# Order of pieces, gate drain and side work in a three-layer fp32 block: one planner, four edits

## The chip, the cores and the metric

One core of a Trainium2 chip. The time is that of one execution on the device, in microseconds (us); the kernel before and the kernel after are compared by the median of their runs.

## The reference

512 tokens of width 1024 pass a layer of dilated attention, a layer of differential attention, and a hybrid block (feed-forward, a mix of sparse attention, state space and memory attention, feed-forward). All is float32. What the change touches:

```python
# first layer: three groups of 16 heads, merged by their log-denominators
alpha = jax.nn.softmax(jnp.stack(lses, axis=0), axis=0)
o = jnp.sum(alpha[..., None] * jnp.stack(outs, axis=0), axis=0)
y = o.reshape(B, S, DIL_WIDTH) * jax.nn.silu(gate)
return y @ w_out                                # 1024 x 1024
# second layer: eight heads of width 128
o = rmsnorm(o, subln) * (1.0 - lambda_init)
y = o.reshape(B, S, DIFF_WIDTH) * jax.nn.silu(gate)
return y @ w_out                                # 1024 x 1024
# hybrid block, of the memory tokens alone
mem_kv = rms_norm(mem, mem_norm[l]) @ w_mem_kv[l]
```

Each layer ends with `h = h + rmsnorm(y, norm_post)`, and the next one normalises `h` again.

## The kernel before, in words

A planner (`make_plan`, with `Plan` from line 100 on) writes one list of jobs. Each engine walks the same list in order and does its own part of each job, so the order of the list is the order of the work on every queue; semaphores tie the engines together.

**Panels, steps, pieces.** A dense product is a *panel* of 512 output columns in four PSUM banks (`panel`, L135). Its weights come in *pieces* of two 128-row chunks (`piece`, L121), 0.5 MB each. A *step* takes two pieces, and has one `mac` job for each of the four banks (token blocks or feature blocks); every yield of the generator is one `mac`. The layers' inputs and these weights are split into a high and a low fp32r part, and a product is three matmuls: high by high, high by low, low by high. So one `mac` of a step of two pieces is 12 matmuls.

**The way of a piece.** SyncE loads it into one of four slots of `raw_ring` (`sync_program`, L1053), once the piece four before has been lowered, or, if that one is not split, once its step has ended. ScalarE rounds it into `hi_ring` (L2173) when the step that used that place of the ring has ended; GpSimd lowers it, that is, subtracts and writes `lo_ring` (L2530). Both do this at fixed places of the job list: the `mac` with the bank `look_at` of each step, up to piece number `ahead` (the pieces planned so far plus `look`).

**End of the first layer** (`dilated_layer`, L365). Under the gate's two panels runs a side stream of attention, loads and the first tile's weights; it is advanced 2.5 places a `mac` (`interleave`, L174). `first_heads` (L443) ends with the jobs `mix_ratio`, `mix_weight` and `mix_scale` of token tile 0. A gate bank is drained by ScalarE's tanh (L2180) and VectorE (L1530). Then for each token tile: VectorE computes the groups' weights (L1658 to L1671), scales two of three groups (L1678; for tile 0 all three) while ScalarE scales the third in 20 operations (L2398), sums the groups (L1688, L1690) and multiplies with the gate (L1695); TensorE transposes the tile (L1130, 8 matmuls); ScalarE rounds it (L2256) and VectorE lowers it (L1601). The projection's first panel takes one token block per tile. Between them TensorE does the memory's product with `w_mem_kv` (`memory_products`, L482; plain fp32, L1222), in four steps of one unsplit piece, and `warm` jobs: matmuls of constants whose result nobody reads (L1424). Each plain fp32 matmul shows as two records.

**End of the second layer** (`differential_layer`, L504). Attention heads are weighed by VectorE (L1749), transposed on TensorE (`turn_head`, L1433), rounded by ScalarE (L2428) and lowered by VectorE (L1755). Heads 0 to 3 come ahead of the projection's first step (K chunks 0 to 3), heads 4 to 7 between its four `mac` jobs; the second step waits for all of them.

**Side work of the first feed-forward** (`before_hybrid`, L611): 62 places that are advanced one a `mac` in ten hidden panels (80 `mac` jobs): memory's keys (L1232), the bias table (L1238), its DMA to and from memory (L2622, L2650) and eight bias heads (L1272), coefficient and table parts on VectorE, state-space tables (L1252, L1260), eight placement DMAs (L2630).

Of the kernel before, what the change touches and what calls it, by code (L numbers as in the profile page):

```python
# [12 lines left out]
NT = S // P  # L13
KC = D // P
KP = 2
# [69 lines left out]
MEM_LOOK = 2  # L85
VALUE_LEAD, HEAD_RATIO = 3, 2.0

Job = namedtuple("Job", "kind at n use")
# [5 lines left out]
class Plan:  # L94
# [23 lines left out]
        self.jobs.append(Job(kind, at, n, use))  # L118
        return use

    def piece(self, w, k0, kq, c0, n, parted, halves, wide):  # L121
        slot = len(self.pieces) % RAW
        self.slot_landed[slot] += 16 * halves
        home, prior = None, None
        if parted and wide is None:
            home = self.n_ring % SPLIT
            prior, self.last_of[home] = self.last_of[home], len(self.steps)
            self.n_ring += 1
        elif parted:
            home = SPLIT + wide  # L130
        self.pieces.append(Piece(w, k0, kq, c0, n, parted, self.n_split, len(self.steps), halves, self.slot_landed[slot], home, prior))
        self.n_split += 1 if parted else 0
        return len(self.pieces) - 1

    def panel(self, kind, w, c0, cols, form, at=(), K=KC, src="x", k_first=0, halves=1, after=(), base=0, late=((),) * 4,  # L135
              wide=(), look=(2, 2, 2), look_at=(0, 0, 0), order=None, needs=None):
        parted = src in ("x", "hidden")
        pi, n = len(self.panels), self.count["panel", kind]
        self.count["panel", kind] += 1
        use = tuple(self.fill(base + b) for b in range(4))  # L140
        if needs is not None:
            pass
        elif src != "x":
            needs = (after,) * 4
        elif form == "feature":
            needs = (tuple(v for part in self.parts for v in part),) * 4
        else:
            needs = self.parts
        self.panels.append(Panel(kind, at, n, w, cols, K, form, src, use, needs, base, late))
        for first in range(0, K, 2 * KP):  # L150
            s, last = len(self.steps), first + 2 * KP >= K
            pieces = [self.piece(w, k_first + k, min(KP, K - k), c0, cols, parted, halves, wide[k // KP] if wide else None)
                      for k in (first, first + KP) if k < K]
            if last:
                end = (f"filled{base + 3}", use[3])
            else:
                self.n_step += 1
                end = ("stepped", self.n_step)
            m = first // (2 * KP)
            self.steps.append(Step(pi, pieces, first, last, end, len(self.pieces) + look[m], look_at[m]))  # L160
            for b in range(4 if order is None else 0):
                self.job("mac", s, b)
                yield MAC_TIME if parted else RAW_TIME
# [201 lines left out]
def dilated_layer(plan, begun):  # L365
# [77 lines left out]
    def first_heads():  # L443
        plan.job("mix_load")
        for m in range(FIRST_HEADS):
            if m % 2 == 0 and m < 8:
                plan.job("mem_weigh", m // 2)
            yield
        plan.job("mix_ratio", 0)
        plan.job("mix_weight", 0)  # L450
        plan.job("mix_scale", 0)

    interleave(gate_panels(plan, w, 9 * D, 0), chain(side, first_heads()), GATE_RATIO)
    plan.job("row", "post0")
    plan.job("gain", "pre1")
    needs = [(), (), (), ()]
    main = plan.panel("y", "dil_w_out", 0, 512, "tile", at=(0,), look=(2, 6), look_at=(2, 0), needs=needs)
    memory = memory_products(plan)
    for n in range(NT):
        if n + 1 < NT:  # L460
            plan.job("mix_ratio", n + 1)
        plan.job("mix_sum", n)
        if n + 1 < NT:
            plan.job("mix_weight", n + 1)
        if n < 2:
            next(memory)
# [15 lines left out]
def memory_products(plan):  # L482

    for first in range(0, KC, KP):
        p = plan.piece("w_mem_kv", first, KP, 0, 512, False, 1, None)
        s, last = len(plan.steps), first + KP >= KC
        use = tuple(plan.fill(b) for b in (2, 3)) if first == 0 else use
        if last:
            end = ("filled3", use[1])
        else:  # L490
            plan.n_step += 1
            end = ("stepped", plan.n_step)
        plan.steps.append(Step(None, [p], first, last, end, len(plan.pieces) + MEM_LOOK, 0))
        plan.job("mem_kv", s, use)
        if last:
            plan.job("mem_out", use)
        yield
# [6 lines left out]
def differential_layer(plan):  # L504
# [52 lines left out]
    def turn_head(h):  # L557
        return ((f"drained{4 + h % 4}", plan.job("o_turn", h, banks=(4 + h % 4,))[0]),)
# [51 lines left out]

def before_hybrid(plan):  # L611
    plan.job("mem_fetch")
    for _ in range(3):
        yield
    for n in range(2):
        plan.job("mem_keep", n)
        yield
        yield
        plan.job("mem_keys", n, banks=(6,))
        yield  # L620
    plan.job("bias_table", banks=(4, 5))
    yield
    plan.job("coefficients")
    for i in range(COEF_PARTS):
        plan.job("coef_part")
# [6 lines left out]
    for _ in range(TABLE_PARTS):  # L632
        plan.job("table_part")
        yield
    for _ in range(4):
        yield
    for f in range(2):
        plan.job("k_make", f, banks=(4, 5))
# [183 lines left out]
def program(nc, I, out):  # L822
    ctx = ExitStack()
    with ctx:  # L824
# [250 lines left out]
        def tensor_program(T):  # L1075
# [4 lines left out]
            def mac(s, b, half=None):  # L1080
# [1701 lines left out]
```

## Time and profile before

| | |
|---|---|
| median of 3 runs | 2210.07 us (2203.17 to 2214.13) |
| the profiled execution | 2206.05 us |
| its span, first to last instruction | 2204.2 us |
| mean granted TensorE clock | 0.989 |
| TensorE busy | 2117.1 us |
| VectorE, ScalarE, GpSimd busy | 967.0, 866.5, 840.0 us |

PE is TensorE's matmul, DVE VectorE, ACT ScalarE, POOL GpSimd, SP SyncE. Times in timelines are us from the span's start. In a timeline a row is one instruction or a run of like ones: start, duration from the first start to the last end, engine, line, operation, output and input names, shapes and number; in brackets the idle time of the engine just before it and what ended that. The ends of matmuls are modelled. A granted clock of 1.00 is 2.4 GHz, 0.50 is 1.2 GHz.

### The profile page before, as it was taken

How to read it: one execution, taken by the hardware profiler on the slowest of the kernel's cores; microseconds unless marked ns; L12 is line 12 of the kernel's file. 1: busy time of each engine (PE TensorE's matmuls, PEld its weight loads, DVE VectorE, ACT ScalarE, POOL GpSimd, SP SyncE). 2: the span in 40 equal slices, each digit the busy share in tenths (PEclk: the TensorE clock that was granted, in tenths of full speed). 3: DMA queues.
4: the chain of work that ended last, by engine and by line, in shares of the span. 5: the costliest groups of instructions: out<-in, count | busy, mean ns of one | idle time of the engine just before them, and what ended most of it. 6: DMA issues, size and time to landing. Idle time of an engine off the chain costs nothing. (4 is left out here: it accounts for less than half of the span.)

```text
span 2204.2 us, 26734 instructions
## 1 busy us (share of the span) xinstructions
PE 2117.1 (96%) x10366; PEld 1684.7 (76%) x10366; DVE 967.0 (44%) x1642; ACT 866.5 (39%) x1769; POOL 840.0 (38%) x447
## 2 busy tenths in 40 slices
PE   8999999999899999989999999999999899999998
PEld 6788888887658767678778888787774478888886
DVE  2444645444444575654571311258666532111211
ACT  4554556564344565543331232333322232221221
POOL 4433233332333323353444445344333152444442
PEclk9999999999999999999999999999999999999999
DMA  6313233232622212132433333233344242323321
GB/s 220 96 58 96 58 96 97 77 97 78 222 92 73 88 58 77 51 122 77 134 96 107 90 101 105 83 93 99 104 149 130 85 153 67 96 96 96 96 96 58
DMA packets 130204, 218.67 MB, mean 99 GB/s; under 512 B 8712, under 2 KB 58552, under 8 KB 129872
## 3 DMA queue, kind: packets, MB, share of 16 engines
q1 hardware_dynamic: 111152, 169.68, 25.3%
q0 software_dynamic: 8096, 28.93, 4.1%
q10 hardware_dynamic: 10832, 18.35, 2.4%
q8 instruction: 84, 1.38, 0.3%
q14 instruction: 40, 0.33, 0.0%
HBM read 198.29 MB, written 18.04 MB: 98 GB/s over the span
## 5 line engine op out<-in xcount | busy, mean ns | idle before, releaser
L2530 POOL TENSOR_TENSOR lo_ring<-raw_ring,hi_ring 128x1024 fp32r<-128x1024 f32 (+1 forms) x288 | 694.5, 2434 | 1009.2 <-ACT hi_ring L2173 1009.1
L1117 PE MATMUL bank<-xh,hi_ring 128*128 128x512 f32 (+1 forms) x1568 | 610.7, 389 | 3.6 <-DVE xl L1601 2.9
L1117 PE MATMUL bank<-xh,lo_ring 128*128 128x512 f32 (+1 forms) x1568 | 593.9, 379 | 0.0
L1117 PE MATMUL bank<-xl,hi_ring 128*128 128x512 f32 (+1 forms) x1568 | 592.6, 378 | 0.0
L2173 ACT CAST hi_ring<-raw_ring 128x1024 fp32r<-128x1024 f32 (+1 forms) x288 | 288.1, 1045 | 406.5 <-PE bank L1117 385.3
L1117 PEld LDWEIGHTS bank<-xh,hi_ring 128*128 128x128 f32 x1568 | 297.1, 189 | 66.2 <-issue 13.8
L1117 PEld LDWEIGHTS bank<-xh,lo_ring 128*128 128x128 f32 x1568 | 296.5, 189 | 56.4
L1117 PEld LDWEIGHTS bank<-xl,hi_ring 128*128 128x128 f32 x1568 | 297.2, 190 | 52.7 <-issue 2.2
L1117 PE MATMUL bank<-hi_ring,xh 128*128 128x512 f32 (+1 forms) x512 | 209.4, 409 | 9.7 <-DVE xl L1755 4.9
L1117 PE MATMUL bank<-hi_ring,xl 128*128 128x512 f32 (+1 forms) x512 | 201.5, 394 | 0.0
L1117 PE MATMUL bank<-lo_ring,xh 128*128 128x512 f32 (+1 forms) x512 | 201.2, 393 | 0.0
L2187 ACT COPY arena<-bank 32x512 f32<-32x512 f32 x256 | 148.1, 579 | 63.1 <-DVE arena L1539 60.4
L1545 DVE SCALAR_TENSOR_TENSOR arena<-arena,bank 128x512 f32<-128x512 f32 x44 | 30.1, 686 | 256.4 <-ACT arena L2204 256.4
L1117 PEld LDWEIGHTS bank<-hi_ring,xh 128*128 128x128 f32 x512 | 105.1, 205 | 34.7 <-issue 14.1
L1564 DVE SCALAR_TENSOR_TENSOR x<-bank,x 128x512 f32<-128x512 f32 x40 | 27.7, 691 | 232.1 <-PE bank L1117 232.1
L1117 PE MATMUL bank<-hi_ring,hidden_hi 128*128 128x512 f32 x320 | 127.0, 397 | 0.0
L1117 PE MATMUL bank<-lo_ring,hidden_hi 128*128 128x512 f32 x320 | 126.8, 396 | 0.0
L1117 PE MATMUL bank<-hi_ring,hidden_lo 128*128 128x512 f32 x320 | 126.8, 396 | 0.0
L1117 PEld LDWEIGHTS bank<-hi_ring,xl 128*128 128x128 f32 x512 | 105.2, 205 | 18.0
L1117 PEld LDWEIGHTS bank<-lo_ring,xh 128*128 128x128 f32 x512 | 105.6, 206 | 15.7 <-issue 0.2
L2538 POOL TENSOR_TENSOR small<-small,minus_half 128x1 f32<-128x1 f32 (+2 forms) x48 | 40.2, 838 | 162.2 <-DVE small L1606 122.1
L2287 ACT COPY arena<-bank 128x512 f32<-128x512 f32 (+6 forms) x97 | 49.3, 508 | 86.6 <-PE bank L1272 21.2
(289 smaller groups left out, 2675.2 us busy)
## 6 DMA issues: line engine op xcount, KB each, us to landing
raw_ring<-in_ffn_w_in SPq DMA_DIRECT2D x176, 256.0 KB, 3.1
raw_ring<-in_dil_w_in SPq DMA_DIRECT2D x80, 512.0 KB, 3.6
raw_ring<-in_ffn_w_out SPq DMA_DIRECT2D x44, 512.0 KB, 3.7
raw_ring<-in_diff_w_in SPq DMA_DIRECT2D x32, 512.0 KB, 3.7
raw_ring<-in_w_in SPq DMA_DIRECT2D x32, 512.0 KB, 3.6
arena<-scratch_heads POOLq DMA_DIRECT2D x4, 1584.0 KB, 12.0
scratch_gates<-arena ACTq DMA_DIRECT2D x24, 256.0 KB, 2.0
arena<-scratch_gates POOLq DMA_DIRECT2D x24, 256.0 KB, 5.0
```

What stands on the lines that cost most here:

```text
L1117: ins = T.matmul(bank[pb][:, cols if p.form == "feature" else slice(0, p.cols)], lhsT, rhs, start=(k == 0 and m == 0 and half != 1), stop= ...
L1545: V.scalar_tensor_tensor(ff_e[:, o, :], ff_e[:, o, :], 1.0, psum, ALU.add, ALU.mult).then_inc(drained[o], 1)
L1564: V.scalar_tensor_tensor(dst, psum, 0.25 if p.kind == "down" else 0.5, dst, ALU.mult, ALU.add).then_inc(drained[o], 1)
L2173: A.copy(split_home(q)[0][:, 0:q.kq * q.n], raw_ring[:, p % RAW, 0:q.kq * q.n]).then_inc(rounded, 1)
L2187: ins = A.copy(rope_b[32 * quad:32 * quad + 32, o % 2, :], psum[32 * (quad ^ 1):32 * (quad ^ 1) + 32, :])
L2287: A.copy(dst, src).then_inc(drained[b], 1)
L2530: G.tensor_tensor(lo, raw_ring[:, p % RAW, 0:q.kq * q.n], hi.bitcast(F32), ALU.subtract).then_inc(lowered, 1)
L2538: G.tensor_tensor(dst, dst, minus_half[:, 0:dst.shape[-1]], ALU.pow).then_inc(made_, 1)
```

## The change

Four edits of the job list. (1) The projection's first two pieces of the first layer are planned ahead of memory's four (`ready`, with their step number given), memory's steps no longer look two pieces ahead, and the `warm` jobs shrink from 5, 9 and 9 matmuls (tiles 0, 2, 3) to 4 and 4 (tiles 2, 3). (2) `mix_scale` of tile 0 comes after the gate's last drain. (3) The side work of the feed-forward gets more empty places. (4) In the second layer heads 2 and 3 are weighed at steps 20 and 21 (were 21 and 23), the projection's first panel has four steps of one piece (two heads) with waits by step, and two `mac` jobs of the first two heads go between the later transposes.

```diff
@@ piece, panel
-    def piece(self, w, k0, kq, c0, n, parted, halves, wide):
+    def piece(self, w, k0, kq, c0, n, parted, halves, wide, step=None):
+        step = len(self.steps) if step is None else step
@@
-              wide=(), look=(2, 2, 2), look_at=(0, 0, 0), order=None, needs=None):
+              wide=(), look=(2, 2, 2), look_at=(0, 0, 0), order=None, needs=None, ready=None, per=2):
@@
-        for first in range(0, K, 2 * KP):
-            s, last = len(self.steps), first + 2 * KP >= K
+        for first in range(0, K, per * KP):
+            s, last = len(self.steps), first + per * KP >= K
             pieces = [self.piece(w, k_first + k, min(KP, K - k), c0, cols, parted, halves, wide[k // KP] if wide else None)
-                      for k in (first, first + KP) if k < K]
+                      for k in range(first, min(K, first + per * KP), KP)] if ready is None or first else ready
@@ dilated_layer
-        plan.job("mix_scale", 0)
 
     interleave(gate_panels(plan, w, 9 * D, 0), chain(side, first_heads()), GATE_RATIO)
+    plan.job("mix_scale", 0)
     plan.job("row", "post0")
     plan.job("gain", "pre1")
     needs = [(), (), (), ()]
-    main = plan.panel("y", "dil_w_out", 0, 512, "tile", at=(0,), look=(2, 6), look_at=(2, 0), needs=needs)
+    ready = [plan.piece("dil_w_out", k, KP, 0, 512, True, 1, None, len(plan.steps) + KC // KP) for k in (0, KP)]
+    main = plan.panel("y", "dil_w_out", 0, 512, "tile", at=(0,), look=(2, 6), look_at=(2, 0), needs=needs, ready=ready)
@@
-        if n != 1:
-            plan.job("warm", n, 4 + 2 * (n % 2), 5 if n == 0 else 9)
+        else:
+            plan.job("warm", n, 4 + 2 * (n % 2), 4)
@@ memory_products
-        plan.steps.append(Step(None, [p], first, last, end, len(plan.pieces) + MEM_LOOK, 0))
+        plan.steps.append(Step(None, [p], first, last, end, len(plan.pieces), 0))
@@ differential_layer
-        if step >= 17 and step % 2:
-            plan.job("o_weigh", (step - 17) // 2)
+        if step in (17, 19, 20, 21):
+            plan.job("o_weigh", (17, 19, 20, 21).index(step))
+    ready = [turn_head(h) for h in range(3)]
+    plan.job("o_lower", 0)
     run_all(side)
+    ready.append(turn_head(3))
+    for h in range(1, 4):
+        plan.job("o_lower", h)
@@
-    ready = [turn_head(h) for h in range(4)]
-    for h in range(4):
-        plan.job("o_lower", h)
     for h in range(4, 8):
         plan.job("o_weigh", h)
-    plan.parts = (sum(ready, ()),) * NT
-    late = [(), (), (), ()]
-    main = plan.panel("y", "diff_w_out", 0, 512, "tile", at=(0,), late=late, look=(2, 6))
+    plan.parts = (ready[0] + ready[1],) * NT
+    late = {2: ready[2] + ready[3]}
+    main = plan.panel("y", "diff_w_out", 0, 512, "tile", at=(0,), late=late, look=(2, 2, 4, 6), look_at=(0, 0, 0, 0), per=1)
     ready = []
     for h in range(4, 8):
-        next(main)
+        for _ in range(2 if h < 6 else 1):
+            next(main)
         ready.append(turn_head(h))
         plan.job("o_lower", h)
-    late[:] = [sum(ready, ())] * NT
+    late[4], late[6] = ready[0] + ready[1], ready[2] + ready[3]
@@ before_hybrid: yields
 mem_fetch, then          3 -> 8
 mem_keep, then           2 -> 3   (for each of two)
 bias_table, then         1 -> 3
 last table part, then    4 -> 8
@@ mac
-                    for name_value in p.late[b]:
+                    for name_value in (p.late.get(st.k0, ()) if isinstance(p.late, dict) else p.late[b]):
```

## Rows read from the trace of the kernel before

**Rows 1.** The page, part 1: busy us, share of the span, instructions.
```profile
PE 2117.1 (96%) x10366; PEld 1684.7 (76%) x10366; DVE 967.0 (44%) x1642; ACT 866.5 (39%) x1769; POOL 840.0 (38%) x447
```
**Rows 2.** TensorE's waits, whole span: us in total, times, longest.
```profile
PE bank L1272 <- DMA arena<-scratch_bias: 3.0, 2, 2.3
...
PE bank L1232 <- DVE arena L1767: 1.0, 1, 1.0
```
**Rows 3.** Timeline of TensorE, end of the first layer.
```profile
597.22 9.56 PE L1222 MATMUL bank<-raw_ring,arena 128*128 128x512 f32 x16 [4.67 <-DVE arena L1530]
606.62 4.46 PE L1424 MATMUL bank<-consts 128*128 128x512 f32 x10
...
611.78 7.03 PE L1222 MATMUL bank<-raw_ring,arena 128*128 128x512 f32 x16
...
622.83 0.77 PE L1117 MATMUL bank<-hi_ring,xh 128*128 128x512 f32 x1 [3.14 <-POOL lo_ring L2530]
...
638.88 7.88 PE L1424 MATMUL bank<-consts 128*128 128x512 f32 x18
646.60 1.04 PE L1130 MATMUL bank<-consts,arena 128*128 128x128 f32 x8
```
**Rows 4.** Windows: stretch, length, busy us (records) by engine, granted clock, DMA, GB/s.
```profile
597.20:606.60 9.40, 9.38 (x16) 4.07 (x17) 7.33 (x14) 5.12 (x21) 0.00 (x0) 0.74 0.80 302
622.80:627.50 4.70, 4.36 (x12) 3.06 (x13) 4.60 (x6) 1.20 (x5) 3.19 (x1) 0.65 0.60 176
...
940.00:963.30 23.30, 17.05 (x83) 13.45 (x82) 16.58 (x31) 9.26 (x21) 6.99 (x6) 0.93 0.28 91
963.30:974.30 11.00, 10.97 (x48) 9.12 (x49) 0.81 (x2) 6.18 (x10) 11.00 (x5) 1.00 0.51 150
```
**Rows 5.** Timeline of VectorE, end of the first layer.
```profile
592.98 3.50 DVE L1678 TENSOR_TENSOR arena<-arena,small 128x1024 f32<-128x1024 f32 x3
596.39 0.68 DVE L1530 SCALAR_TENSOR_TENSOR arena<-arena,bank 128x512 f32<-128x512 f32 x1
...
600.74 1.22 DVE L1695 SCALAR_TENSOR_TENSOR arena<-arena 128x1024 f32<-128x1024 f32 x1
...
605.83 0.24 DVE L1658 TENSOR_REDUCE small<-arena 128x16 f32<-128x48 f32 x1 [1.87 <-issue]
...
613.73 1.22 DVE L1695 SCALAR_TENSOR_TENSOR arena<-arena 128x1024 f32<-128x1024 f32 x1
...
620.52 3.25 DVE L1690 TENSOR_TENSOR arena<-arena 128x1024 f32<-128x1024 f32 x1
```
**Rows 6.** Timeline of ScalarE, end of the first layer.
```profile
600.86 4.88 ACT L2398 ACTIVATE arena<-arena,small 128x64 f32<-128x64 f32 x20 [3.08 <-DVE small L1671]
611.55 1.07 ACT L2256 CAST xh<-bank 128x512 fp32r<-128x512 f32 x2 [5.81 <-PE bank L1130]
```
**Rows 7.** GpSimd's timeline there, and one DMA row (KB, us to landing).
```profile
582.42 3.12 POOL L2590 DMA_DIRECT2D arena<-scratch_heads  x4 [6.09 <-DMA scratch_heads<-arena]
...
619.76 6.23 POOL L2530 TENSOR_TENSOR lo_ring<-raw_ring,hi_ring 128x1024 fp32r<-128x1024 f32 x2 [33.10 <-ACT hi_ring L2173]
...
arena<-in_rows POOLq DMA_DIRECT2D x1, 512.0 KB, 17.5
```
**Rows 8.** Timeline of TensorE, end of the second layer.
```profile
946.25 0.47 PE L1117 MATMUL bank<-hi_ring,xh 128*128 128x512 f32 x1 [3.14 <-DVE xl L1755]
...
963.33 0.47 PE L1117 MATMUL bank<-hi_ring,xh 128*128 128x512 f32 x1 [1.77 <-DVE xl L1755]
```
**Rows 9.** Timeline of VectorE, end of the second layer.
```profile
943.28 2.73 DVE L1755 SCALAR_TENSOR_TENSOR xl<-bank,small,xh 128x512 fp32r<-128x512 f32 x4 [0.40 <-ACT xh L2428]
945.92 8.52 DVE L1749 SCALAR_TENSOR_TENSOR arena<-arena,small 128x128 f32<-128x128 f32 x16
```
**Rows 10.** Timeline of TensorE, first feed-forward: a bias head.
```profile
1086.56 1.81 PE L1272 MATMUL bank<-arena,consts 128*128 128x512 f32 x2 [2.27 <-DMA arena<-scratch_bias]
```
**Rows 11.** Timeline of GpSimd, first feed-forward: loads for bias heads.
```profile
1080.25 1.09 POOL L2650 DMA_DIRECT2D arena<-scratch_bias  x2
```

More of the change, by code:

```diff
@@ L84 @@
 MAC_TIME, RAW_TIME = 2.7, 1.7
-MEM_LOOK = 2
 VALUE_LEAD, HEAD_RATIO = 3, 2.0
@@ L124, in piece @@
         home, prior = None, None
+        step = len(self.steps) if step is None else step
         if parted and wide is None:
             home = self.n_ring % SPLIT
-            prior, self.last_of[home] = self.last_of[home], len(self.steps)
+            prior, self.last_of[home] = self.last_of[home], step
             self.n_ring += 1
@@ L130, in piece @@
             home = SPLIT + wide
-        self.pieces.append(Piece(w, k0, kq, c0, n, parted, self.n_split, len(self.steps), halves, self.slot_landed[slot], home, prior))
+        self.pieces.append(Piece(w, k0, kq, c0, n, parted, self.n_split, step, halves, self.slot_landed[slot], home, prior))
         self.n_split += 1 if parted else 0
@@ L149, in panel @@
         self.panels.append(Panel(kind, at, n, w, cols, K, form, src, use, needs, base, late))
-        for first in range(0, K, 2 * KP):
-            s, last = len(self.steps), first + 2 * KP >= K
+        for first in range(0, K, per * KP):
+            s, last = len(self.steps), first + per * KP >= K
             pieces = [self.piece(w, k_first + k, min(KP, K - k), c0, cols, parted, halves, wide[k // KP] if wide else None)
-                      for k in (first, first + KP) if k < K]
+                      for k in range(first, min(K, first + per * KP), KP)] if ready is None or first else ready
+            assert all(self.pieces[q].step == s for q in pieces)
             if last:
@@ L158, in panel @@
                 end = ("stepped", self.n_step)
-            m = first // (2 * KP)
+            m = first // (per * KP)
             self.steps.append(Step(pi, pieces, first, last, end, len(self.pieces) + look[m], look_at[m]))
@@ L162, in panel @@
                 self.job("mac", s, b)
-                yield MAC_TIME if parted else RAW_TIME
+                yield (MAC_TIME if parted else RAW_TIME) * per / 2
         for m, b, *half in order or ():
@@ L550, in differential_layer, with turn_head @@
             next(side, None)
-        if step >= 17 and step % 2:
-            plan.job("o_weigh", (step - 17) // 2)
+        if step in (17, 19, 20, 21):
+            plan.job("o_weigh", (17, 19, 20, 21).index(step))
+    def turn_head(h):
+        return ((f"drained{4 + h % 4}", plan.job("o_turn", h, banks=(4 + h % 4,))[0]),)
+    ready = [turn_head(h) for h in range(3)]
+    plan.job("o_lower", 0)
     run_all(side)
+    ready.append(turn_head(3))
+    for h in range(1, 4):
+        plan.job("o_lower", h)
     plan.job("row", "post1")
     plan.job("gain", "ffn1")
-    def turn_head(h):
-        return ((f"drained{4 + h % 4}", plan.job("o_turn", h, banks=(4 + h % 4,))[0]),)
-    ready = [turn_head(h) for h in range(4)]
-    for h in range(4):
-        plan.job("o_lower", h)
     for h in range(4, 8):
         plan.job("o_weigh", h)
-    plan.parts = (sum(ready, ()),) * NT
-    late = [(), (), (), ()]
-    main = plan.panel("y", "diff_w_out", 0, 512, "tile", at=(0,), late=late, look=(2, 6))
+    plan.parts = (ready[0] + ready[1],) * NT
+    late = {2: ready[2] + ready[3]}
+    main = plan.panel("y", "diff_w_out", 0, 512, "tile", at=(0,), late=late, look=(2, 2, 4, 6), look_at=(0, 0, 0, 0), per=1)
     ready = []
     for h in range(4, 8):
-        next(main)
+        for _ in range(2 if h < 6 else 1):
+            next(main)
         ready.append(turn_head(h))
         plan.job("o_lower", h)
-    late[:] = [sum(ready, ())] * NT
+    late[4], late[6] = ready[0] + ready[1], ready[2] + ready[3]
     run_all(main)
@@ L612, in before_hybrid @@
     plan.job("mem_fetch")
-    for _ in range(3):
+    for _ in range(8):
         yield
@@ L616, in before_hybrid @@
         plan.job("mem_keep", n)
-        yield
-        yield
+        for _ in range(3):
+            yield
         plan.job("mem_keys", n, banks=(6,))
@@ L621, in before_hybrid @@
     plan.job("bias_table", banks=(4, 5))
-    yield
+    for _ in range(3):
+        yield
     plan.job("coefficients")
@@ L634, in before_hybrid @@
         yield
-    for _ in range(4):
+    for _ in range(8):
         yield
```

## The prediction

> **What bounds the kernel now.** I first read the busy line of the page [rows 1]: TensorE works for 96% of the span, no other engine for over half. So time comes back only where TensorE waits, where it runs slowly, or where it computes something that nobody needs. The list of TensorE's waits names the operation behind each; two of its rows lie in the feed-forward whose side work the diff spreads [rows 2]. The rest I take from timelines, first that of the first layer's end [rows 3]. It waits 4.67 us for the drain of the last gate bank, 3.14 us for the lowered piece of the projection, and between them it issues filler products: 10 records for 4.46 us, and twice 18 records for 7.88 us. The windows [rows 4] show the clock: 1.00 is the 2.4 GHz level; a mean of 0.74 over 9.4 us and of 0.65 over 4.7 us is 1.2 GHz for about 4.9 and 3.3 us of them, each right behind one of the two long waits. The timelines of VectorE, ScalarE and GpSimd [rows 5 to 7] then say whether anything would be ready for TensorE if the filler were gone.
>
> **Part A, end of the first layer.** I walk it from 592.55 (597.22 - 4.67), when the gate panel's last product ends.
>
> Last bank first. Before, the scale of tile 0 (3.50 us) stands ahead of the gate's drain, which starts at 596.39 [rows 5]. After, the drain needs only ScalarE's tanh (about 0.6 us) and its own 0.68 us: 593.9. The first two memory pieces start at 594.0, not 597.2. Their 16 records took 9.56 us at the mixed clock and 7.03 us at full clock [rows 3]. With a wait of 1.4 us in place of 4.67 us I take 7.03: they end at 601.0 (before: 606.6). What is late next is VectorE's sum, since the scale only changed places: tile 0 was mixed at 600.74 + 1.22 and is so 0.25 us later, 602.2. TensorE waits 1.2 us, turns the tile (0.9 us), and does the other two memory pieces (7.0 us): 610.1. The filler of 4.46 us in between is gone.
>
> The chain under it. Before, the mixed tiles come 13 us apart, 600.74 and 613.73 [rows 5]. The chain's own work is shorter: ScalarE's 20 scalings 4.88 us [rows 6], the ratio that starts at their end (605.83) about 0.5, two sums 2.4 (1.17 each, from the scale's row), and the weights 1.1 (from ScalarE's end at 612.62 to 613.73): 8.9 us. The other 4 us are ScalarE, in order, waiting 5.81 us at the rounding of tile 0 for a transpose that stood behind memory and filler on TensorE [rows 6]. With the transpose at 602.2 that wait is gone. So tiles 1, 2 and 3 are mixed at about 611.1, 620.0 and 628. Behind tile 1 VectorE scales (2.1) and lowers tile 0 (1.3): 614.4.
>
> The projection's pieces. Before, they are rounded behind the second memory step, lowered from 619.76, and TensorE starts on them at 622.83 [rows 3, 7]. After, they stand ahead of memory's: the last gate step's look-ahead of two covers them, ScalarE rounds them when their ring slots come free (592.55 less 48 products at 0.228, 581.6), and GpSimd lowers them behind its four loads of heads, which end at 585.54 [rows 7]; two took 6.23 us in their old place, so by 591.8 they are done. SyncE is moved past too: memory's third and fourth piece need these lowerings, so they are issued near 588.7 and 591.8 amid 6.3 MB of heads and 1 MB of rows. Bounds: at least nothing; a transfer of 0.5 MB among those took 17.5 us [rows 7], so at most the third lands at 606.2, 3.1 us late for a need at 603.1. The 2.4 us wait found below, right behind, absorbs all but 0.7 of that, so I take 0. The two broadcast rows that GpSimd issues some 5 to 6 us later are first used tens of us on.
>
> The lowering's new place meets gate drains on VectorE. In its old place an addition of 1.17 us took 3.25 [rows 5]. By that row alone three drains could each be 2 us late, and one of them would count: 0 to 2 us. I take 0, as the drains are short and come 2.7 us apart. The Trainium skill, page "SBUF — State Buffer", section "Who interferes with whom", says that a VectorE operation with two SBUF inputs and a GpSimd operation that reads SBUF keep each other out, while one with a single SBUF input does not. By it the drain, whose other input is a bank, loses nothing.
>
> The end of part A. One token block of one step is 12 products, 2.74 us (a quarter of 10.97 [rows 4]). Block 0 of the projection: 614.4 to 617.1. Filler of 4 now (8 records, 3.5 us): 620.6; transpose: 621.5; block 1 needs the lowered tile 1, 614.4 + 8.9 = 623.3, so a wait of 1.8; 626.0; filler 629.5; transpose 630.4; blocks 2 and 3: 635.9. Before: transpose at 646.60, blocks 2 and 3 end at 652.9. That is 17.0 us, 13.2 of it the 15 filler products (4.46 + 2 x 4.38). Part A keeps waits of 1.2, 2.4 and 1.8 us; if the clock falls once behind the 2.4 us, half of about 3.4 us is lost, partly inside the next wait. I take 16, between 12 and 18.
>
> **Part B, end of the second layer.** Before, TensorE waits for all four lowerings of heads 0 to 3 (2.73 us from 943.28) and starts at 946.25; its next step waits 1.77 us for the last of heads 4 to 7, to 963.33, and takes 10.97 us: 974.3 [rows 4, 8, 9]. After, the first step has two heads. ScalarE's rounding of head 0 stands behind the squares of the last head as before, so head 0 is lowered at 943.95 and head 1 at 944.8: a start 1.4 us earlier. From there 96 products at 0.228 (21.9) and four transposes of heads (2.4) run to 969.2. VectorE's 16 weighings took 8.52 us [rows 9], 0.53 each, and the first four now start at 946.2 and end near 948.3 against a need at 947.6: 0.7 us. The clock fell behind the 3.14 us wait here too (a mean of 0.93 over 23.3 us, half of 3.3 us [rows 4]); behind 2.8 us I let it fall half the time, 0.9. End: 970.8, so 3.5 us gained; bounds 2 and 5. The weighing of heads 2 and 3 two steps earlier fills idle VectorE time (its next gate drain is tied to ScalarE's tanh); if that cover were gone it would cost its own 1.1 us.
>
> **Part C, side work in the feed-forward.** Waits of 1.0 (memory's keys) and 3.0 us (bias heads) [rows 2], the largest 2.27 us [rows 10]. The load of bias 3 is issued at 1080.25 [rows 11] because in GpSimd's order it stands directly behind the lowering of a step's pieces; its use comes three blocks on and the load takes about 6 us. The new yields (8 before, 3 for 2, 3 for 1) move the loads by nine places, that is from directly behind the lowerings to one block further, and each use then comes one block (2.7 us) later after the lowering. 2.7 covers 2.27 and 0.78. The keys get three blocks where they had two; but the first one's root on GpSimd now stands behind a lowering, so I keep 0.2 of the 1.0. The clock's fall behind the 2.27 us wait (about 1.7) goes as well. Side places used rise from 62 to 75 of 80, so nothing spills; eight placement transfers on GpSimd come with three blocks before the next lowering where there were four, and TensorE has no wait there. Sum 5.3; I take 5, bounds 2.5 and 6.
>
> **Sum.** 16 + 3.5 + 5 = 24.5 us; by the bounds 16.5 to 29. The profiled execution took 2206.05 us (span 2204.2), 4 us under the median 2210.07. From the one 2181.5, from the other 2185.6: I take **2183**.
>
> **Rivals.** *R1: the chain stays at 13 us.* If the scalings and sums need the old distance, tile 3 is lowered near 637, blocks 2 and 3 end at 644, and part A gives 9: about 2192 from the median. For it: VectorE's order holds four kinds of work in a row. Against: the 5.81 us wait of ScalarE is released by TensorE.
>
> *R2: the clock falls behind every wait that is left.* Five waits of 1.2 to 2.8 us, each with 6.8 us at 1.2 GHz as behind the 4.67 us one, cost 3.4 each, 17 in all: about 2202, no change that can be told. For it: [rows 4]. Against: behind the 1.77 us wait the clock stayed at 1.00 [rows 4, 8].
>
> *R3: slower.* The filler is what holds the clock between the transposes. Without 15 of 23 it could stay at 1.2 GHz from 594 through the projection: 36.8 us of work become 73.6, its end 667.6 against 652.9, and the second step adds 11: 25.7 us lost, 8.5 given back by B and C: 2227. It decides from 49 us at 1.2 GHz on (24.5 x 2); the longest stretch behind a wait here was about 7. The Trainium skill, page "TensorE: Matmul & The Clock Gate", Part 1, says that the slow level is the default and that activity releases it, which speaks for this rival; the trace agrees as far as both long waits go, and it also shows the clock back at full speed while only memory's products and filler ran.
>
> *The change doesn't do what it says*, if the pieces are not rounded at the gate's last step but behind the memory products: then block 0 starts near 620 and part A gives 11, about 2191; its chance is in R1's.
>
> **Chances.** Forecast 0.76, R1 0.14, R2 0.07, R3 0.03. About 0.5%, 11 us, is what a measurement can tell from no change: the first two are faster by more, R2 is the same, R3 slower. The range reaches from the lowest run of before less the upper bound (2203.2 - 29 = 2174) past R1 to 2198.
>
> **What would show it.** Right: 8 filler products; the memory products starting under 2 us behind the last gate product; mixed tiles 9 us apart; the projection's first block near 614, waiting for a lowered tile and not for GpSimd; the second layer's projection starting some 1.4 us earlier relative to the transposes and never waiting over 1 us; no wait over 1 us at the bias heads. Wrong: tiles still 13 us apart, clock means under 0.9 over 20 us, or new waits for memory's transfers.

## The result and the profile after

The changed kernel takes 2185.86 us (median of 4 runs, 2183.25 to 2190.55) against 2207.83 us (median of 4); the ratio is 0.9895 with a 95% interval of 0.9872 to 0.9919. That is 22.0 us less by the medians. Its profiled execution took 2186.33 us, span 2184.5, so 19.7 us less than the 2204.2 of before.

The changed kernel's lines are numbered six higher from the planner on: L1130 is now L1136, L1117 L1123, L1222 L1228, L1424 L1430, L1433 L1439.

TensorE's timeline of the changed kernel, end of the first layer (answers to [rows 3]):

```profile
594.52 7.10 PE L1228 MATMUL bank<-raw_ring,arena 128*128 128x512 f32 x16 [1.50 <-DVE arena L1536]
602.73 1.09 PE L1136 MATMUL bank<-consts,arena 128*128 128x128 f32 x8 [1.10 <-DVE arena L1701]
603.65 7.03 PE L1228 MATMUL bank<-raw_ring,arena 128*128 128x512 f32 x16
611.57 1.09 PE L1136 MATMUL bank<-consts,arena 128*128 128x128 f32 x8 [0.89 <-DVE arena L1701]
614.82 0.47 PE L1123 MATMUL bank<-hi_ring,xh 128*128 128x512 f32 x1 [2.15 <-issue]
...
617.64 3.59 PE L1430 MATMUL bank<-consts 128*128 128x512 f32 x8
...
623.73 0.47 PE L1123 MATMUL bank<-hi_ring,xh 128*128 128x512 f32 x1 [1.61 <-DVE xl L1607]
...
626.55 3.59 PE L1430 MATMUL bank<-consts 128*128 128x512 f32 x8
629.98 1.04 PE L1136 MATMUL bank<-consts,arena 128*128 128x128 f32 x8
...
647.25 0.63 PE L1123 MATMUL bank<-wide_ring,xh 128*128 128x512 f32 x2
```

The last row is the first product of the projection's second panel, 663.85 before. Every wait is there that the walk had, within 0.3 us; none of them waits for GpSimd or for a transfer. For the 2.15 us one the profile names no releaser (`issue`); VectorE's lowering of tile 0, 613.44 to 614.72 in the rows below, ends just ahead of the block's start at 614.82. VectorE's timeline of the changed kernel (answers to [rows 5]): a drain beside GpSimd's lowering, the last drain ahead of the scale, and mixed tiles that now start 8.85 us apart in place of 13:

```profile
588.25 0.69 DVE L1536 SCALAR_TENSOR_TENSOR arena<-arena,bank 128x512 f32<-128x512 f32 x1 [2.03 <-ACT arena L2186]
...
593.69 0.69 DVE L1536 SCALAR_TENSOR_TENSOR arena<-arena,bank 128x512 f32<-128x512 f32 x1 [0.27 <-ACT arena L2186]
594.29 3.49 DVE L1684 TENSOR_TENSOR arena<-arena,small 128x1024 f32<-128x1024 f32 x3
...
601.45 1.22 DVE L1701 SCALAR_TENSOR_TENSOR arena<-arena 128x1024 f32<-128x1024 f32 x1
...
610.30 1.22 DVE L1701 SCALAR_TENSOR_TENSOR arena<-arena 128x1024 f32<-128x1024 f32 x1
...
613.44 1.28 DVE L1607 TENSOR_TENSOR xl<-bank,xh 128x512 fp32r<-128x512 f32 x2
...
619.16 1.22 DVE L1701 SCALAR_TENSOR_TENSOR arena<-arena 128x1024 f32<-128x1024 f32 x1
```

ScalarE rounds tile 0 the moment its scalings end, where it waited 5.81 us [rows 6], and GpSimd lowers the projection's pieces right behind the loads of heads [rows 7]. One row of each timeline:

```profile
606.36 1.04 ACT L2262 CAST xh<-bank 128x512 fp32r<-128x512 f32 x2
```

```profile
585.84 4.76 POOL L2536 TENSOR_TENSOR lo_ring<-raw_ring,hi_ring 128x1024 fp32r<-128x1024 f32 x2
```

Windows of the changed kernel (columns as in [rows 4]): the clock holds through the first layer's end with 8 filler products, and falls in the feed-forward at a place where it did not fall before (there it fell at a bias head, at 1086 us):

```profile
594.50:636.40 41.90, 36.12 (x129) 21.50 (x130) 32.19 (x47) 24.16 (x77) 3.68 (x2) 1.00 0.46 174
...
1253.00:1265.00 12.00, 12.00 (x56) 8.99 (x56) 1.38 (x2) 1.77 (x3) 0.00 (x0) 0.72 0.16 44
```

The reason is a new wait, at the state-space table's first product. TensorE's timeline of the changed kernel, second layer (answers to [rows 8]), then that product:

```profile
930.92 0.77 PE L1123 MATMUL bank<-hi_ring,xh 128*128 128x512 f32 x1 [2.87 <-DVE xl L1761]
...
935.61 0.66 PE L1439 MATMUL bank<-consts,arena 128*128 128x128 f32 x4 [0.32 <-DVE arena L1755]
...
1253.00 4.54 PE L1258 MATMUL bank<-consts,arena 64*16 64x128 f32 x32 [1.46 <-DVEq L1883]
```

**A ledger by stretches.** Single executions of one kernel differ by up to 13 us on one chip (before: 2197.68 to 2210.93), and by 18 over all its executions, but the time between two marks on TensorE's timeline repeats closely wherever the clock does the same: A within 0.1 us, C within 0.2, M within 0.5.

I use four stretches. A: from the last gate product to the first product of the projection's second panel (54.23 = 647.25 - 593.02 after). M: from there to the first head's transpose, work that no edit is meant to touch (u10 and u11 move the transpose that ends it). B: from there to the second layer's second panel. C: from there to the first transpose behind the feed-forward.

| kernel | A | M | B | C |
|---|---|---|---|---|
| before | 71.30 | 276.28 | 34.20 | 409.38 |
| after | 54.23 | 278.80 | 30.53 | 407.70 |
| difference | -17.07 | +2.52 | -3.67 | -1.68 |

Together -19.9, against 19.7 less in the whole span. M is the clock: 6.8 and 3.4 us at 1.2 GHz stand behind two of its waits after, 3.4 behind one before. Its waits are the same within 0.1 us but for the first, 0.82 us before and 0.18 after, which differs from execution to execution (0.60 in another one of the changed kernel); without that the clock took 3.2, not 2.5. The same kernel in `after_again` (below), with 3.4 us behind one wait, has M at 276.09, below the 276.28 of before.

### The profile page after: what moved, and what is told of

Its sections match the earlier page's. It is cut to its first block and busy times, and to the rows that moved or that the text cites. A ratio compares the mean times of both kernels' runs of the same rounds, so it can differ in the third digit from the quotient of the medians.

```text
span 2184.5 us, 26673 instructions
## 1 busy us (share of the span) xinstructions
PE 2103.2 (96%) x10336; PEld 1680.2 (77%) x10336; DVE 955.9 (44%) x1642; ACT 866.1 (40%) x1769; POOL 837.4 (38%) x447
## 5 line engine op out<-in xcount | busy, mean ns | idle before, releaser
L1123 PE MATMUL bank<-xh,hi_ring 128*128 128x512 f32 (+1 forms) x1568 | 610.9, 390 | 3.5 <-DVE xl L1607 2.9
L1123 PE MATMUL bank<-xh,lo_ring 128*128 128x512 f32 (+1 forms) x1568 | 594.1, 379 | 0.0
L1123 PE MATMUL bank<-xl,hi_ring 128*128 128x512 f32 (+1 forms) x1568 | 592.8, 378 | 0.0
L1123 PEld LDWEIGHTS bank<-xh,hi_ring 128*128 128x128 f32 x1568 | 297.1, 190 | 66.3 <-issue 13.8
L1123 PEld LDWEIGHTS bank<-xh,lo_ring 128*128 128x128 f32 x1568 | 296.6, 189 | 56.2
L1123 PEld LDWEIGHTS bank<-xl,hi_ring 128*128 128x128 f32 x1568 | 297.4, 190 | 52.4 <-issue 1.9
L1123 PE MATMUL bank<-hi_ring,xh 128*128 128x512 f32 (+1 forms) x512 | 209.6, 409 | 8.2 <-DVE xl L1761 2.9
L1123 PE MATMUL bank<-hi_ring,xl 128*128 128x512 f32 (+1 forms) x512 | 201.4, 393 | 0.0
L1123 PE MATMUL bank<-lo_ring,xh 128*128 128x512 f32 (+1 forms) x512 | 201.3, 393 | 0.0
L1123 PEld LDWEIGHTS bank<-hi_ring,xh 128*128 128x128 f32 x512 | 105.4, 206 | 32.6 <-issue 12.7
L1123 PE MATMUL bank<-hi_ring,hidden_hi 128*128 128x512 f32 x320 | 127.0, 397 | 0.0
L1123 PE MATMUL bank<-hi_ring,hidden_lo 128*128 128x512 f32 x320 | 126.9, 397 | 0.0
L1123 PE MATMUL bank<-lo_ring,hidden_hi 128*128 128x512 f32 x320 | 126.9, 396 | 0.0
L1123 PEld LDWEIGHTS bank<-hi_ring,xl 128*128 128x128 f32 x512 | 105.2, 205 | 17.8
L1123 PEld LDWEIGHTS bank<-lo_ring,xh 128*128 128x128 f32 x512 | 105.8, 207 | 15.7 <-issue 0.2
L1545 DVE TENSOR_TENSOR arena<-bank,consts 128x512 f32<-128x512 f32 x64 | 44.0, 687 | 92.6 <-PE bank L1123 91.4
```

The costliest lines, as they stand in the source:

```text
L1123: ins = T.matmul(bank[pb][:, cols if p.form == "feature" else slice(0, p.cols)], lhsT, rhs, start=(k == 0 and m == 0 and half != 1), stop= ...
L1545: V.tensor_tensor(rope_a[:, o % 2, :], psum, const("cos"), ALU.mult).then_inc(cosed, 1)
```

## The experiments

Each is the changed kernel with one edit, if not said otherwise, and has one profiled execution. The ratio is that of its median to the median of the kernel before, run beside it. The stretches:

| kernel | A | M | B | C |
|---|---|---|---|---|
| u1_old_yields | 54.21 | 276.29 | 30.54 | 407.40 |
| u2_tables_11 | 54.23 | 277.94 | 30.56 | 403.15 |
| u3_filler_back | 60.97 | 277.57 | 30.55 | 404.49 |
| u4_no_filler | 52.77 | 277.53 | 31.44 | 404.50 |
| u5_memory_first | 59.27 | 277.51 | 30.54 | 407.72 |
| u6_scale_first | 53.99 | 277.77 | 30.57 | 404.50 |
| u7_four_heads | 54.26 | 277.75 | 34.18 | 404.55 |
| after_again | 54.21 | 276.09 | 30.56 | 404.53 |
| tables_11_again | 54.19 | 276.31 | 30.57 | 402.99 |
| u9_both | 52.85 | 277.44 | 30.31 | 402.98 |
| u10_early_heads | 52.86 | 276.45 | 30.33 | 402.98 |
| u11_weigh_first | 52.78 | 274.82 | 28.24 | 402.99 |

### What the filler is worth

```diff
-        else:
-            plan.job("warm", n, 4 + 2 * (n % 2), 4)
+        if n != 1:
+            plan.job("warm", n, 4 + 2 * (n % 2), 5 if n == 0 else 9)
```

> The changed kernel with the old filler of 5, 9 and 9 products. It leaves everything else, so it parts the filler from the order of the pieces. Theory (the walk of part A): the filler's 13.2 us come back, but where TensorE waited before (1.1, 0.9, 2.2, 1.6 us) they are hidden: the first block of the projection stays near 615 to 616, the last block of its first step ends near 643.5 in place of 636.3, so 7 us slower than the changed kernel, near 2193. Rival, that the filler was the whole gain and the order of pieces worth nothing: 13 us slower, near 2199.

Ratio to before 0.9937 (0.9919 to 0.9955), median 2192.28. A is 60.97, 6.7 us more, as the theory had it (7) and not 13. The filler costs its 13.2 us less the waits that it hides. The first five products cost nothing: the first block waits 0.29 us in place of 2.15 and starts 21.80 us behind the last gate product with them and without. The second block no longer waits at all.

```profile
603.39 4.45 PE L1430 MATMUL bank<-consts 128*128 128x512 f32 x10
...
616.75 0.47 PE L1123 MATMUL bank<-hi_ring,xh 128*128 128x512 f32 x1 [0.29 <-issue]
619.60 7.89 PE L1430 MATMUL bank<-consts 128*128 128x512 f32 x18
```

The other side, no filler (the two lines with `else:` and `warm` go):

> The changed kernel with no filler product at all. Theory: VectorE and ScalarE mix a tile each 8.9 us, so TensorE only waits where it computed filler; the projection's first step ends 1 to 1.6 us earlier if the clock stays at 2.4 GHz, and each stretch of 3.4 us at 1.2 GHz that the longer waits (4 to 5 us) bring costs up to 1.7: between 1.5 us faster and 4 us slower than the changed kernel. Rival, that the filler holds the clock up for the whole projection: the clock's mean from 595 to 660 falls below 0.8 and the span is over 10 us longer.

Ratio 0.9895 (0.9863 to 0.9926), median 2181.31. A is 52.77, 1.5 us less than the changed kernel, though the clock fell for 6.8 us at the longest wait. (B is 0.9 longer, for a fall of 6.8 us of its own.) TensorE's timeline, and the clock's mean over the stretch in a window:

```profile
620.22 1.97 PE L1134 MATMUL bank<-consts,arena 128*128 128x128 f32 x8 [2.64 <-DVE arena L1699]
623.51 0.77 PE L1121 MATMUL bank<-hi_ring,xh 128*128 128x512 f32 x1 [1.33 <-DVE xl L1605]
```

```profile
594.30:645.60 51.30, 42.99 (x161) 29.14 (x162) 32.16 (x47) 27.96 (x81) 14.96 (x7) 0.93 0.53 186
```

0.93, not under 0.8 (from 595 to 660 it is 0.95): the fall costs little, because TensorE is waiting for VectorE anyway. The rival that the filler holds the clock up for the whole projection is out. That is R3 of the prediction.

### What the order of the pieces is worth

```diff
-    ready = [plan.piece("dil_w_out", k, KP, 0, 512, True, 1, None, len(plan.steps) + KC // KP) for k in (0, KP)]
-    main = plan.panel(..., needs=needs, ready=ready)
+    main = plan.panel(..., needs=needs)
@@ memory_products
-        plan.steps.append(Step(None, [p], first, last, end, len(plan.pieces), 0))
+        plan.steps.append(Step(None, [p], first, last, end, len(plan.pieces) + 2, 0))
```

> The changed kernel with the projection's first two pieces planned behind memory's four again and the look-ahead of two in memory's steps; the filler stays at 4 and 4 and the scale behind the drain. It parts the order of the pieces from the filler. From the last gate product to the first product of the projection's second panel the changed kernel took 54.2 us, the one before 71.3. Theory: the pieces are rounded only behind ScalarE's second group of 20 scalings (near 615) and lowered by 618 to 620, so the first block starts at 618.5 to 620 in place of 614.8 with a wait of 5 to 8 us; VectorE's sum of tile 2 meets the lowering and is 2 to 4 us later; the stretch takes 59 to 63 us. Rival, that the pieces' order is worth nothing once the filler is cut: 54 to 55.5 us.

One execution: 2188.17 us. A is 59.27, 5.0 more, inside the 59 to 63 of the theory. TensorE's timeline shows the wait back, and VectorE's shows the sum at 3.25 us again (as in [rows 5]) while GpSimd lowers from 616.38; its tile 2 is mixed at 623.41, 4.25 us later than after. The sum is 2.0 us of that; a small operation behind it, which also reads two SBUF tiles beside the lowering, took 2.41 us in place of 0.24.

```profile
619.45 0.76 PE L1122 MATMUL bank<-hi_ring,xh 128*128 128x512 f32 x1 [6.73 <-POOL lo_ring L2535]
```

```profile
617.14 3.25 DVE L1695 TENSOR_TENSOR arena<-arena 128x1024 f32<-128x1024 f32 x1
620.31 2.41 DVE L1670 TENSOR_TENSOR small<-small,arena 128x48 f32<-128x48 f32 x1
...
623.41 1.22 DVE L1700 SCALAR_TENSOR_TENSOR arena<-arena 128x1024 f32<-128x1024 f32 x1
```

With u3 this splits A's 17.1: the filler gives 6.7 with the new order and 12.0 (71.30 - 59.27) with the old, the order 5.0 with the short filler and 10.3 (71.30 - 60.97) with the long. The two figures with old settings hold the drain's move as well, whose worth there no run measures. Neither sum of single effects is 17.1; the filler hid part of the late pieces, and the other way round.

### What the drain's move is worth

```diff
+        plan.job("mix_scale", 0)
 
     interleave(gate_panels(plan, w, 9 * D, 0), chain(side, first_heads()), GATE_RATIO)
-    plan.job("mix_scale", 0)
```

> The changed kernel with the scaling of tile 0 ahead of the gate's last drain again. It parts the drain's move from the rest. Theory: the first memory products start 3.2 to 3.5 us later (a wait of 4.7 us) and run partly at 1.2 GHz, but what is late next is not memory: the first block of the projection waits 2.15 us for a lowering that VectorE makes at the same time as before, and the second 1.6 us. So most of it is absorbed: the stretch from the last gate product to the second panel takes 54.2 to 56.5 us, and the drain's move is worth at most 2 us of the 17. Rival: it is worth its 3.2 us and the clock's 2.5 in full, and the stretch takes 59 to 60 us.

Nothing, with the new order and the short filler: one execution, 2184.83 us, A 53.99, 0.2 us under the changed kernel's; the rival's 59 to 60 is out. The wait of 4.68 us is back, 3.4 us of the memory products run at 1.2 GHz, and yet the second block starts 30.5 us behind the last gate product, as it does after (30.7).

```profile
597.73 8.61 PE L1228 MATMUL bank<-raw_ring,arena 128*128 128x512 f32 x16 [4.68 <-DVE arena L1536]
...
617.57 3.59 PE L1430 MATMUL bank<-consts 128*128 128x512 f32 x8
621.00 1.04 PE L1136 MATMUL bank<-consts,arena 128*128 128x128 f32 x8
623.52 0.47 PE L1123 MATMUL bank<-hi_ring,xh 128*128 128x512 f32 x1 [1.49 <-DVE xl L1607]
```

### The second layer in steps of four heads

The edit puts the old text of `differential_layer` back from the weighings on.

```diff
-        if step in (17, 19, 20, 21):
+        if step >= 17 and step % 2:
...
-    main = plan.panel("y", "diff_w_out", 0, 512, "tile", at=(0,), late=late, look=(2, 2, 4, 6), look_at=(0, 0, 0, 0), per=1)
+    main = plan.panel("y", "diff_w_out", 0, 512, "tile", at=(0,), late=late, look=(2, 6))
```

> The changed kernel with the end of the second layer as before (steps of four heads, weighings at steps 17, 19, 21 and 23). Theory: from the first transpose of a head to the second panel's first product the time goes back from 30.5 to 34.2 us with the waits of 3.1, 0.5 and 1.8 us, and nothing else in the span moves by over 0.3 us but for stretches at 1.2 GHz; the kernel is 3.7 us slower than the changed one. Rival, that the earlier pieces of the next panel or VectorE's order gave the gain and not the two-head steps: the waits come back but the stretch stays under 32.

Ratio 0.9923 (0.9907 to 0.9940), median 2189.51. B is 34.18 with the waits of before to the hundredth, so the rival (under 32) is out; A is unmoved. The run takes back the whole edit: what the earlier weighings alone are worth, and what the steps of two heads, is not shown.

```profile
933.24 0.47 PE L1120 MATMUL bank<-hi_ring,xh 128*128 128x512 f32 x1 [3.14 <-DVE xl L1758]
...
950.30 0.47 PE L1120 MATMUL bank<-hi_ring,xh 128*128 128x512 f32 x1 [1.77 <-DVE xl L1758]
```

### The side work of the feed-forward

The old empty places (3, 2, 2, 1, 4):

> The changed kernel with the side work of the feed-forward spaced as before (3, 2, 2, 1 and 4 empty places). Between two marks on TensorE's timeline, the projection's last panel of the second layer and the first transpose behind the feed-forward, the changed kernel gained only 1.7 us on the one before. Theory: the spread saved some 5.5 us there (waits of 1.0, 2.3 and 0.8 and a stretch at 1.2 GHz behind them) and brought a new wait of 1.5 us at the first table product with 6.8 us at 1.2 GHz behind it, about 4.9 us. So this kernel should show the waits at the bias heads again and none at the table product, and its span should be 1 to 3 us longer than 2184.5. Rival (the prediction's own term, and the new wait a chance of that run): 5 us longer or more.

Ratio 0.9903 (0.9875 to 0.9930), median 2184.94. Waits of 1.25 us at the keys and of 1.30, 0.36 and 0.56 at bias heads are back, the table product waits for nothing, and C is 407.40. The theory compared with the profile at 2184.5 and missed: the span came out shorter (2177.7), not longer, and C is 0.3 under that profile's 407.70. That profile's C holds a fall of the clock. Of the seven executions with the eight new places five have C at 404.5, and against these C is 2.9 us longer, as the theory had it in kind. The other two, the changed kernel's first profile and u5, have 407.7, and only in these the clock fell behind the table product's wait, for 6.8 us: such a fall costs 3.2 us. The wait's own price is 1.5 us, 404.5 less the 403.0 of the kernels with 11 places (403.15 in the next run).

```diff
         plan.job("table_part")
         yield
-    for _ in range(8):
+    for _ in range(11):
         yield
```

> The changed kernel with 11 empty places ahead of the table products in place of 8, so that the first of them stands behind a block of a panel's first step and not of its last. Theory: the table product waited 1.5 us because VectorE signals the tables only behind the drain of that last step's bank; moved three places on it waits for nothing, the clock stays up, and the span falls by about 4.9 us, to 2179 to 2181. Rival: the wait comes from the tables' own work on VectorE, which is now later by ten places; then it stays (1 to 1.5 us) wherever the product stands, and the span does not change by over 1 us.

Ratio 0.9876 (0.9851 to 0.9901), median 2177.68, C 403.15. The product waits for nothing. That alone would not exclude the rival, since the product also comes three blocks later; the changed kernel's VectorE does. Its last table part ends at 1235.2; behind that it did only bank drains and lowerings up to 1239.8, and then sat idle for 9.72 us. What the product waited for is a place in VectorE's order: the signal that the tables are done stands at the job of the table product, and with 8 places that job comes behind the drain of a last step's second bank. That drain, with its wait, ends at 1252.89; the product starts at 1253.00.

```profile
1249.48 0.69 DVE L1551 SCALAR_TENSOR_TENSOR arena<-arena,bank 128x512 f32<-128x512 f32 x1 [9.72 <-ACT arena L2210]
1252.20 0.69 DVE L1551 SCALAR_TENSOR_TENSOR arena<-arena,bank 128x512 f32<-128x512 f32 x1 [2.03 <-ACT arena L2210]
```

To compare on one chip, both kernels again:

> The changed kernel itself, beside the others on one chip. Theory: 54.2 us in the first layer's end, 30.5 in the second's, both within 0.2; in the feed-forward 404.5 us where the clock stays up behind the 1.46 us wait of the first table product and 407.7 where it falls. Median near 2184.

> The changed kernel with 11 empty places ahead of the table products, beside the changed kernel on one chip. Theory: the feed-forward's stretch is 403.1 us with no wait at the table product, 1.4 us under the changed kernel's where its clock stays up and 4.6 where it falls, so the median is 1.5 to 5 us lower. Rival: no difference in the medians beyond 1 us, since the earlier one came from another chip.

Ratios to before 0.9881 (0.9853 to 0.9909) and 0.9882 (0.9859 to 0.9906), medians 2181.95 and 2182.72. The stretches of the changed kernel repeat (54.21, 30.56, 404.53). C gives its 1.5 us again (404.53 and 402.99), and the medians give nothing, as the rival had it: 1.5 us is under what whole runs can tell, and the 8.2 us by which u2's median (2177.68) lay under the changed kernel's first (2185.86) are not the edit's alone.

### Can the waits that are left go

In the first layer, lower first and scale behind it, together with the 11 places:

```diff
+        if n:
+            plan.job("lower", n - 1, 4 + 2 * ((n - 1) % 2))
         if n + 1 < NT:
             plan.job("mix_scale", n + 1)
         if n:
-            plan.job("lower", n - 1, 4 + 2 * ((n - 1) % 2))
```

> The changed kernel with two edits: 11 empty places ahead of the table products, and in the first layer VectorE lowers a tile before it scales the next but one (the jobs lower and mix_scale swapped). Theory: the 2.15 and 1.6 us waits of the projection's blocks end at the lowering, which stands behind two scalings of 1.04 us; swapped it comes 2.1 us earlier, and the scaling still ends inside ScalarE's 4.9 us of scalings, so tiles still come 8.9 us apart. The stretch of the first layer's end falls from 54.2 to 52.3 us (then bound by the last mixed tile near 628), and with the tables' 5 us less the span is near 2175. Rival: the scaling on VectorE is what the next sum waits for; then tiles come 10.2 us apart and the stretch takes 56 us or more.

Ratio 0.9890 (0.9875 to 0.9905), median 2181.51. A is 52.85, 1.4 us less (the theory had 52.3), and tiles keep their distance of 8.9 us, so the rival is out: the wait moved from the block to the transpose, that is, to the mixed tile.

```profile
620.10 1.09 PE L1137 MATMUL bank<-consts,arena 128*128 128x128 f32 x8 [1.24 <-DVE arena L1702]
621.39 0.47 PE L1124 MATMUL bank<-hi_ring,xh 128*128 128x512 f32 x1 [0.20 <-DVE xl L1608]
```

In the second layer, on top of that, the transposes of heads 0 to 2 ahead of the last values and squares:

```diff
+        if step == 23:
+            owed -= 1.0
@@ behind the loop: turn_head 0 to 2, o_lower 0 and 1, run_all(side),
@@ one block of the projection, turn_head 3, o_lower 2 and 3, o_weigh 4 to 7
```

> The kernel of the run before with one more edit: in the second layer the transposes and roundings of heads 0 to 2 and the lowerings of heads 0 and 1 stand ahead of the last values and squares of attention, and the first block of the projection stands ahead of head 3's transpose. Theory: the 2.9 us wait of the first block is ScalarE's four squares of head 7 (1.2 us) and VectorE's drain of the last values standing ahead of the roundings; without them the block starts 2 to 3 us earlier, and the stretch from the first head's transpose to the second panel takes 28 to 29 us against 30.5 (it now starts up to 0.9 us earlier as well). Rival: VectorE's weighing of head 4 decides (it waits 1.7 us already where the clock is up), and then the stretch stays within 0.7 us of 30.5.

Ratio 0.9880 (0.9865 to 0.9895), median 2179.58. The rival held: B is 30.33. (The first transpose, M's end, comes 0.9 us earlier; M and B together are 1.0 us under those of u9, in which the clock fell at the same two places.) The first block's wait fell from 2.88 to 0.73 us and came back at head 4's transpose:

```profile
924.62 0.47 PE L1129 MATMUL bank<-hi_ring,xh 128*128 128x512 f32 x1 [0.73 <-DVE xl L1767]
...
930.89 0.66 PE L1445 MATMUL bank<-consts,arena 128*128 128x128 f32 x4 [2.81 <-DVE arena L1761]
```

So head 4's weighing goes ahead as well:

```diff
     for h in range(2):
         plan.job("o_lower", h)
+    plan.job("o_weigh", 4)
     run_all(side)
@@ two blocks of the projection ahead of turn_head 3, then one ahead of each
```

> The kernel with early transposes of heads 0 to 2, the swap of lowering and scaling, and 11 empty places, changed once more: head 4 is weighed ahead of the last values' drain, head 3 is transposed behind the projection's second block, and from there each transpose follows one block. With the transposes alone the wait only moved: 0.7 us at the first block and 2.8 us at head 4's transpose, 30.3 us in all. Theory: the wait is VectorE's weighing of head 4 behind two lowerings; weighed first it is ready, and the stretch takes 27.5 to 28.8 us. Rival: the wait moves on to head 5 (VectorE's 16 weighings and 4 lowerings are its own bound in this stretch), and it stays over 29.5.

Ratio 0.9853 (0.9828 to 0.9877), median 2175.79; B is 28.24, as the theory had it, with two waits of 0.7 us left. It beats both kernels: 6.2 us under the changed one beside it on the same chip (2181.95). By stretch against `after_again` it is 1.4 us in A, 1.3 in M (0.9 of it the earlier transpose, the rest M's first wait, which is gone in this execution), 2.3 in B and 1.5 in C.

## Why the prediction was right, and where it was not

**The total.** 2183 was forecast and 2185.86 measured, a gain of 24.5 by the sum against 22.0; it lies within the range. The profiled executions show how far that was luck: A gave 1.1 us more than its term, B 0.2 more, C 3.3 less, and M took 2.5, which leaves 19.9.

**Part A.** 17.07 against a walk of 17.0, of which I took 16 for a fall of the clock that did not come in this execution. Where it came, it cost nothing: in `after_again`, u2 and u7 the clock fell for 3.4 us at the first block's wait, and A was 54.21, 54.23 and 54.26. The deduction was the part that was wrong. The steps held one by one, counted from the last gate product, which ends 0.47 us later here: memory 594.5, transposes 602.7 and 611.6, blocks 614.8 and 623.7. The walk also holds a wait that its list leaves out, 1.0 us ahead of the second transpose (0.89 measured); with it R3's 36.8 us of work are 35.5, which moves no chance. The chain of 8.9 us between mixed tiles, hidden under a distance of 13, was the step that mattered. The filler's removal and the pieces' order are shown by u3 and u5. One edit of the three did nothing beside the other two, the drain's move (u6, one execution): my walk carried its 3.2 us to the memory products, correctly, and then counted the result only at the end, so it could not show that this part was idle. By R2 and R3 the clock was to fall behind the waits that are left, and to cost 3.4 us each time or far more: in A it fell in some executions and not in others, and in u4, for 6.8 us, it cost less than the filler.

**The lowering's place.** I took 0 of 0 to 2 us for the lowering beside the gate's drains; the one at 588.25, inside the lowering's 585.84 to 590.60, took 0.69 us as the last one did without it. In its old place the sum is slow again (3.25 us in u5, 1.22 after). Both agree with the Trainium skill, page "SBUF — State Buffer", section "Who interferes with whom": the sum has two SBUF inputs, the drain one.

**Part B.** 3.67 against 3.5, shown by u7. The first block starts 4.87 us behind the first transpose, 6.12 before: 1.25 earlier, where I had 1.4. Head 4's transpose waited 0.32 us behind blocks at a clock that had fallen for 3.4 us, and 1.43 to 1.72 in the seven executions with the new steps in which the clock did not fall behind the first block's wait (u1, u2, u3, u6, u9 and the two repeated kernels): I had priced that wait at 0.7 and the fall at 1.7. They stand for each other, and the stretch is 30.5 either way; only the fall of 6.8 us in u4 made it 31.4. My sign that TensorE would wait nowhere over 1 us once the projection runs was wrong where the clock stayed up.

**Part C.** This is the term that failed: 5 was forecast, 1.68 measured. The old waits went as argued, but the sentence "nothing spills", with no wait of TensorE in that place before, was no check of the new place. It counted the places used and the transfers on GpSimd, and did not ask what stands ahead of the table product's signal in VectorE's order. Place 49 was behind a panel's first step, which drains nothing; place 62 is behind a last step. The wait is 1.5 us, and in the profiled execution 3.2 more by the clock. The old waits and the fall behind one of them were worth 6.4 us (409.38 - 403.0), 1.4 more than I took; less 1.5 and 3.2 that is the 1.7. Without the new fall C gives 4.9 (409.38 - 404.5), and that nearness to 5 is luck: two errors that cancel.

**What was no part of it.** M lost 2.5 us, 3.2 to the clock less 0.6 of a shorter first wait.

## What to carry to other kernels

Filler that keeps an engine busy also keeps the next engine waiting for it: before taking a distance between stages for their cost, add up the stage's own work (8.9 us here against 13), and measure the filler by taking it away. When work moves to another place in an order shared by all engines, look at what each engine does just ahead of the new place, above all the one that signals; a count of free places says nothing of it. An edit that takes 3.2 us off the longest wait of a stretch (4.68 us in u6, 1.50 after) can be worth nothing if a later wait for another engine ends at the same time as before.

## What was not expected of the hardware

The clock of TensorE falls or stays up behind the same wait in the same kernel: behind the 1.46 us wait of the table product it stayed up in five executions and fell for 6.8 us in two. Behind the 2.70 us wait in stretch M it fell for 6.8 us after and not at all before or in `after_again`, and for 3.4 us in eight other executions. A fall of 6.8 us cost 3.2 us where TensorE had work without a break (C) and 0.9 in u4's B; one of 3.4 us cost nothing where a wait for VectorE stood right behind it (A, B). That makes whole spans differ by more than most of the edits studied here, and stretches between marks the better measure.
